# Branch projections from high and low parts, with the first gate products among the last head's products, in a two-block transformer kernel

## The chip, the cores and the metric

The kernel runs on one core of one Trainium2 chip. The metric is device time in microseconds of one execution, as the median of several runs on the same chip.

## The reference

A first block (two layers of attention of three kinds and a gated FFN) is followed by a second block with a gated linear attention (GLA) and an mLSTM side by side. All that this change touches lies in the second block, after its scans. Sequence 512, width 1024, all float32:

```python
y_gla = head_rms_norm(o_l, gla_norm_g) * silu(pp[3])
y_m = h * sigmoid(pp[8])                       # pp = split columns of u @ w_in_2
gate_gla, gate_m = split(sigmoid(pp[10]), 2)   # 2 x 1024 columns of u @ w_in_2
y = gate_gla * (y_gla @ w_br_gla) + gate_m * (y_m @ w_br_mlstm)
x = x + g1 * (y @ w_out)
x = x + g2 * swiglu(modulate(rms_norm(x, norm2_g), sh2, sc2), w_ffn_in, w_ffn_out)
return rms_norm(x, final_g)
```

## The kernel before, in words

Features lie on partitions: a 1024 x 512 activation is eight tiles of 128 x 512 (KT = 8). Most matrix products are made in three passes: each operand is split into a high part (rounded to fp32r) and a low part (value minus high), and one product of 8 tiles is 24 matmuls, high x high, high x low and low x high (`parts_steps`, `parts_job`). A product is 128 output features wide. Two products of the kernel in question are made otherwise: the branch products (`job` with raw fp32 weights and raw Y or YM).

Each engine has its own program, and engines meet at semaphores. PE writes into rings of PSUM banks: `ab` (three banks, emptied by ACT) and `db` (two banks, emptied by DVE). `fill` waits until a bank is free, `take` until it is full. `Program.more` waits for the next count of a semaphore, `do` issues an instruction and waits for it.

The mLSTM has four heads, each scanned in two directions (`mlstm_scan` on PE, `mlstm_outputs` on DVE). A scan makes row products (four partitions deep), key transposes, five state products, and four output products. In heads 0 to 2, `nxt` gives generators with the next head's projections, and `mlstm_scan` puts slices of them between its own products (`some(between, 2)`). In the last head `nxt` gives nothing. Y (GLA) and YM (mLSTM) are eight tiles each; head h makes tiles 2h and 2h + 1 of YM in `head_outputs` on DVE.

Weights of the second block come in pieces of 1 MB, in the order of the list `SECOND`, into places of SBUF given by `PLACE`. SP asks for a piece as soon as the last reader of its place has finished (`load_second`). For projection pieces POOL makes the high part (`round_piece`, L798) and DVE the low part (`second_low`, L2410). For the gate pieces and the output pieces POOL makes both (`split_piece`, L780). The raw branch weights have two halves of place 1 (`load_branch`).

After the last head, PE goes over eight output tiles m: gate product, branch product with Y, gate product, branch product with YM. ACT takes the sigmoid of the gate products, DVE multiplies, adds and splits the sum into `BR_HIGH` and `BR_LOW`. Then PE waits for all eight splits and makes the eight output products; DVE adds them to the residual x, ACT squares x, POOL folds the squares, and after the root DVE normalizes x tile by tile for the FFN (`norm_into_parts`), with high parts by ACT and low parts by DVE. For the first FFN weight ACT makes the high part after the root (`second_ffn_inputs`) and POOL the low part (`first_low`); for the second, ACT makes the high part after the eight tiles and DVE the low part.

## Time and profile before

| | |
|---|---|
| median of 3 runs | 2912.88 us (2911.32 to 2922.45) |
| the profiled execution, its own time | 2913.8 us |
| its span, first to last instruction | 2911.9 us |
| mean granted TensorE clock | 0.961 |
| PE busy | 94% of the span |
| DVE, ACT, POOL busy | 47%, 34%, 31% |

The branch stage is the stretch from about 2275 to 2467 us of the span; the last mLSTM head lies before it, from about 2217, and the third FFN starts at about 2532. A busy share is a mean over stages with different limits; the windows and the chain of waits tell them apart. A timeline row merges like instructions that follow each other; its duration is from the first start to the last end.

### The profile page before, as it was taken

The page shows a single profiled execution, that of the slowest core. Times are in us where ns is not written, and L with a number is a line of the kernel's source. Part 1 is how long each engine was busy: PE and PEld are TensorE (multiplying, and loading weights), DVE is VectorE, ACT ScalarE, POOL GpSimd, SP SyncE. Part 2 cuts the span into 40 slices and gives each one's busy share as a digit, 9 for nine tenths or more (in the row PEclk, how much of TensorE's full clock was granted, in tenths as well). Part 3 has the DMA queues.
Part 4 walks back from the last instruction along what each step waited for, and adds up shares of the span by engine and source line. Part 5 has one row for each costly group of instructions (what it writes and reads, how often), then busy time and mean ns, then how long its engine had stood idle before and what let it go on. Part 6 is the DMA issues. An engine that isn't in the chain of part 4 may idle for free.

```text
span 2911.9 us, 35929 instructions
## 1 busy us (share of the span) xinstructions
PE 2724.6 (94%) x14116; PEld 2165.0 (74%) x14116; DVE 1355.0 (47%) x1808; ACT 980.7 (34%) x1650; POOL 896.5 (31%) x674
## 2 busy tenths in 40 slices
PE   7988999999999799999998999898888999899998
PEld 6866788887798577888876767567776565688887
DVE  2748655443345776544434355545444212333332
ACT  5458522222343883222223434332222100222222
POOL 5566513345346553243461100300000223200000
PEclk8999999999999999999998999898997999899999
DMA  5220034554421101454551211011111331233332
GB/s 131 83 60 1 27 98 127 134 143 136 126 81 62 37 1 56 112 152 133 139 151 54 59 44 44 29 38 35 30 44 44 87 87 58 58 108 95 93 90 79
DMA packets 396728, 230.44 MB, mean 79 GB/s; under 512 B 9772, under 2 KB 392876, under 8 KB 396560
## 3 DMA queue, kind: packets, MB, share of 16 engines
q1 hardware_dynamic: 394608, 226.19, 28.1%
q0 software_dynamic: 1952, 1.94, 0.8%
q8 instruction: 113, 1.85, 0.3%
q14 instruction: 55, 0.45, 0.0%
HBM read 226.01 MB, written 2.10 MB: 78 GB/s over the span
## 4 chain that ended last, share of the span: by engine, by line
PE 76%; DVE 9%; ACT 8%; DMA 5%; issue 2%; POOL 1%; SPq 0%; DVEq 0%; ACTq 0%; POOLq 0%
PE ps L840 65%; PE scores L840 8%; DMA raws<-in_w_down 4%; ACT wH L1832 1%; PE ps L982 1%; DVE R L2150 1%; DVE wL L2361 1%; DVE ring_parts L2414 1%; DVE spare L2160 0%; ACT U L1671 0%; ACT R L1970 0%; DMA ring<-in_w_in 0%; DVE QK_parts L2140 0%; ACT spare L1694 0%; ACT R L1671 0%
## 5 line engine op out<-in xcount | busy, mean ns | idle before, releaser
L840 PE MATMUL ps<-xH,wH 128*128 128x512 f32 x1000 | 396.0, 396 | 7.4 <-DVE xL L2335 7.0
L840 PE MATMUL ps<-xL,wH 128*128 128x512 f32 x1000 | 390.9, 391 | 0.0
L840 PE MATMUL ps<-xH,wL 128*128 128x512 f32 x1000 | 390.5, 391 | 0.0
L1832 ACT ACTIVATE wH<-raws 128x2048 fp32r<-128x2048 f32 (+1 forms) x114 | 192.9, 1692 | 494.5 <-PE ps L840 337.0
L2361 DVE TENSOR_TENSOR wL<-raws,wH 128x2048 fp32r<-128x2048 f32 (+1 forms) x113 | 230.2, 2037 | 255.3 <-ACT wH L1832 254.6
L840 PE MATMUL ps<-ring_parts,U_parts 128*128 128x256 f32 (+1 forms) x1968 | 322.1, 293 | 21.5 <-DVE ring_parts L2217 6.2
L840 PEld LDWEIGHTS ps<-ring_parts,U_parts 128*128 128x128 f32 x1968 | 286.8, 200 | 36.8 <-issue 29.8
L840 PE MATMUL ps<-R 128*64 128x128 f32 (+3 forms) x1688 | 246.0, 336 | 32.7 <-DVE R_parts L2171 7.0
L730 POOL TENSOR_TENSOR spare<-spare,cvec 128x1024 f32<-128x1024 f32 x64 | 122.0, 1907 | 436.4 <-DMA spare<-in_w_ada 436.4
L840 PEld LDWEIGHTS ps<-R 128*64 128x64 f32 (+2 forms) x1688 | 159.6, 167 | 117.6 <-issue 62.5
L840 PEld LDWEIGHTS ps<-xH,wH 128*128 128x128 f32 x1000 | 188.8, 189 | 49.6 <-issue 8.0
L840 PE MATMUL ps<-U_parts,ring_parts 128*128 128x512 f32 (+2 forms) x720 | 216.7, 391 | 9.5 <-DVE ring_parts L2414 9.5
L840 PEld LDWEIGHTS ps<-xH,wL 128*128 128x128 f32 x1000 | 188.5, 189 | 39.9
L840 PEld LDWEIGHTS ps<-xL,wH 128*128 128x128 f32 x1000 | 188.9, 189 | 37.9 <-issue 0.5
L803 POOL CAST ring_parts<-ring 128x2048 fp32r<-128x2048 f32 x23 | 45.7, 1986 | 532.2 <-DMA ring<-in_w_in 532.0
L840 PE MATMUL ps<-hH,wH 128*128 128x512 f32 x528 | 209.3, 396 | 0.0
L840 PE MATMUL ps<-hL,wH 128*128 128x512 f32 x528 | 206.3, 391 | 0.0
L840 PE MATMUL ps<-hH,wL 128*128 128x512 f32 x528 | 206.1, 390 | 0.0
L732 POOL TENSOR_TENSOR spare<-spare 128x512 f32<-128x512 f32 (+2 forms) x192 | 188.7, 983 | 15.1
L840 PEld LDWEIGHTS ps<-U_parts,ring_parts 128*128 128x128 f32 (+1 forms) x720 | 132.8, 189 | 45.5 <-DVE ring_parts L2414 10.4
L693 POOL TENSOR_TENSOR ring_parts<-ring,ring_parts 128x2048 fp32r<-128x2048 f32 (+2 forms) x23 | 99.4, 4325 | 147.5 <-ACT ring_parts L1619 147.2
L840 PE MATMUL ps<-ring_parts 128*128 128x512 f32 (+1 forms) x376 | 131.5, 350 | 0.0
(418 smaller groups left out, 4797.4 us busy)
## 6 DMA issues: line engine op xcount, KB each, us to landing
raws<-in_w_gate_up SPq DMA_DIRECT2D x88, 512.0 KB, 5.3
ring<-in_w_in SPq DMA_DIRECT2D x34, 1024.0 KB, 5.8
spare<-in_w_ada SPq DMA_DIRECT2D x64, 512.0 KB, 3.9
raws<-in_w_down SPq DMA_DIRECT2D x32, 704.0 KB, 6.1
raws<-in_w_ffn_in SPq DMA_DIRECT2D x44, 512.0 KB, 5.0
ring<-in_w_in SPq DMA_DIRECT2D x22, 512.0 KB, 5.4
raws<-in_w_ffn_out SPq DMA_DIRECT2D x16, 704.0 KB, 4.6
ring<-in_w_o SPq DMA_DIRECT2D x12, 448.0 KB, 3.7
```

The costliest lines, as they stand in the source:

```text
L693: pg.do(nc.gpsimd.tensor_tensor(low, slot(i, KT, n_), high.bitcast(F32), ALU.subtract), piece_low)
L730: pg.do(nc.gpsimd.tensor_tensor(w_, w_, bc(cvec[:, :, ADA[a][1]], P, 2), ALU.mult))
L732: pg.do(nc.gpsimd.tensor_tensor(w[:, 0:n_ * P], w[:, 0:n_ * P], w[:, n_ * P:2 * n_ * P], ALU.add), ada_summed if n_ == 1 else None)
L803: pg.do(nc.gpsimd.tensor_copy(high, raw_), second_high)
L840: return nc.tensor.matmul(o, a, b, start=first, stop=last)
L982: ins = nc.tensor.transpose(bank[:, s_ * P:(s_ + 1) * P], PX[a % 4][:, c, s_ * P:(s_ + 1) * P], ident[:, :])
L1832: ap.do(f(wH[:, g % 2, 0:n], raws[:, g % 2, 0:n], ACT.Copy), wh_ready)
L2150: vp.do(v.tensor_reduce(nmax[:, n:n + 2], SP[a % 2][:, :, :], AX.X, ALU.max, negate=True), s_max)
L2361: vp.do(v.tensor_tensor(wL[:, g % 2, 0:n], raws[:, g % 2, 0:n], wH[:, g % 2, 0:n].bitcast(F32), ALU.subtract), wl_ready)
L2414: vp.do(v.tensor_tensor(low, raw_, high.bitcast(F32), ALU.subtract), piece_split)
```

## The change

The branch weights become pieces like the others: in `SECOND` a gate piece (`gates`, both branches' gate columns for one m) and a branch piece (columns m of both branch weights) alternate, over three places that were in use for other things before (places 0, 1 and a new place 2 in the region of the context's parts), and the output pieces follow on places 1, 3, 4 and 2. POOL only rounds all of them; DVE makes the low parts at places written out by hand. Y and YM are split: ACT makes the high parts (`y_rounds`), DVE the low parts in place (`y_subtract`), at several points of the last head.

PE's order: the four gate products of m = 0 and 1 become fillers among the last head's products; the first branch product takes the place of the first gate product; then three branch products; then for m = 2 to 7 two gate products and two branch products. The first product of the output stage waits for its tiles one by one. The first FFN weight's high part is made between the squares of tiles 6 and 7, its low part by DVE after the last residual update; the second weight's high part is made ahead of the normalized tiles.

```diff
-        PLACE = [j % 2 for j in range(N_PROJ)] + [(0, 2, 3)[j % 3] for j in range(KT + 4)]
+        SECOND += [(name, m) for m in range(KT) for name in ("gates", "branch")] + [("out", j) for j in range(4)]
+        PLACE = [j % 2 for j in range(N_PROJ)] + [2, 0, 1] + [(2, 1, 0)[j % 3] for j in range(2 * KT - 3)] + [1, 3, 4, 2]
...
@@ POOL @@
-            for j in range(SECOND.index(("gate", NH2)), N_PROJ):
+            for j in range(SECOND.index(("gate", NH2)), len(SECOND)):
                 round_piece(j)
-            for j in range(N_PROJ, len(SECOND)):
-                split_piece(j)
...
             fold_squares()
-            first_low(L)
...
@@ PE @@
+            def last_fillers(name, m=0):
+                filler = {("v", 1): (0, 0), ("v", 3): (0, 1), ("v", 4): (1, 0), ("gate", 0): (1, 1)}.get((name, m))
+                return branch_gates(*filler) if filler else iter(())
+
+            def branch(m, n):
+                columns = late_columns("branch", m, n)
+                own = m < 2 and n == 0
+                bank = SP[1][:, m, :] if own else db.fill(pe)
+                for k in range(KT):
+                    if m == 0:
+                        pe.wait_ge(y_split, n * KT + k + 1)
+                    (ah, al), (_, bh, bl) = columns(k), y_parts(n * KT + k)
+                    mm(bank[:, :], ah, bh, k == 0, False)
+                    mm(bank[:, :], ah, bl, False, False)
+                    ins = mm(bank[:, :], al, bh, False, k == KT - 1)
...
-                    nxt = projections(NH2 + h + 1) if h + 1 < NH2 else no_projections
+                    nxt = projections(NH2 + h + 1) if h + 1 < NH2 else last_fillers
...
-                    branch_gates(0, 0)
+                    branch(0, 0)
                 head_outputs()
-            pp.more(y_ready, 2 * NH2)
-            for m in range(KT):
-                if m > 0:
-                    branch_gates(m, 0)
-                pe.wait_ge(br_in[m % 2], 32 * (m // 2 + 1))
-                job(db, lambda b: b[:, :], [(branch_raw(m, 0)[:, k, :], Y[:, k, :]) for k in range(KT)])
-                branch_gates(m, 1)
-                job(db, lambda b: b[:, :], [(branch_raw(m, 1)[:, k, :], YM[:, k, :]) for k in range(KT)])
-                branch_read.append((d_full, db.n))
-            pp.more(br_ready, KT)
+            branch(1, 0)
+            branch(0, 1)
+            branch(1, 1)
+            for m in range(2, KT):
+                for n in range(2):
+                    run(branch_gates(m, n))
+                for n in range(2):
+                    branch(m, n)
             for m in range(KT):
+                j = SECOND.index(("out", m // 2))
+                parts_job(db, lambda b: b[:, :], late_columns("out", m // 2, m % 2), lambda k: (BR_HIGH[:, k, :], BR_LOW[:, k, :]),
+                          (lambda: pp.more(br_ready)) if m == 0 else None)
@@ ACT @@
                 for k in range(KT):
                     square(k)
+                    if k == KT - 2:
+                        split_high(L, 0)
                 root()
-                split_high(L, 0)
+                split_high(L, 1)
                 for k in range(KT):
                     high_tile(xH[:, k, :], k)
-                split_high(L, 1)
...
@@ ACT, after the last head @@
+            y_rounds(KT + 2, KT + 5)
+            for m in range(2):
+                ap.do(f(first_gates[m][0], first_gates[m][0], ACT.Sigmoid), gate_ready)
+            act.wait_ge(y_ready, 2 * NH2)
+            y_rounds(KT + 5, 2 * KT)
...
 DVE, mlstm_outputs(h, d), last head
+                    y_subtract(4 * d, 4 * d + 2)
                 vp.more(wexp_ready)
...
+                    if d == 1:
+                        second_low("branch", 0)
+                    y_subtract(4 * d + 2, 4 * d + 4)
                 states(mlstm_order(d), STm, DV + 1, lambda c: dec[:, d, c:c + 1])
...
@@ DVE, loop over heads @@
+                else:
+                    second_low("gates", 0)
                 for d in range(2):
                     mlstm_outputs(h, d)
+                    if h + 1 == NH2 and d == 0:
+                        second_low("gates", 1)
                 vp.also(og_ready)
+                    second_low("branch", 1)
+                    y_subtract(KT, KT + 2)
+                    head_outputs(h, 4, YM, lambda: y_subtract(KT + 2, KT + 5))
+                    y_subtract(KT + 5, 2 * KT)
...
@@ DVE, branch and output stage @@
                 split(BR_HIGH[:, m, :], BR_LOW[:, m, :], PTb[:, 0, :], br_ready)
+                if m >= 1 and m + 1 < KT:
+                    second_low("branch", m + 1)
+                    second_low(*(("gates", m + 2) if m + 2 < KT else ("out", 0)))
+            second_low("out", 1)
...
+                if m in (1, 3):
+                    second_low("out", 2 + m // 2)
+                if m == KT - 1:
+                    split_low(L, 0)
             ffn_norm(L, lambda k: gm[:, 2, k:k + 1], lambda k: mod[:, sh2 + k, 0:1])
```

## Rows read from the trace of the kernel before

**Rows 1.** The page, section 4: the chain that ended last, by engine.

```profile
PE 76%; DVE 9%; ACT 8%; DMA 5%; issue 2%; POOL 1%; SPq 0%; DVEq 0%; ACTq 0%; POOLq 0%
```

**Rows 2.** Windows: stretch, length, busy PE PEld DVE ACT POOL, granted clock, DMA, GB/s.

```profile
2133.00:2217.00 84.00, 74.98 (x395) 61.22 (x393) 36.56 (x78) 20.79 (x37) 10.73 (x4) 0.92 0.14 39
2217.00:2265.00 48.00, 40.98 (x129) 28.02 (x129) 19.59 (x51) 8.39 (x12) 0.00 (x0) 0.61 0.16 43
2548.00:2910.00 362.00, 354.18 (x1584) 293.39 (x1584) 127.35 (x127) 87.05 (x79) 0.00 (x0) 0.99 0.32 92
```

**Rows 3.** Chain of waits, branch and output stage: start, us, engine, line.

```profile
2306.60 5.45 PE scores L840 x24
...
2459.90 6.88 PE ps L840 x16
...
2467.64 4.50 DVE R L2631
...
2473.36 46.07 PE ps L840 x192
```

**Rows 4.** PE in time, last head: start, us, line, operation, count [idle before].

```profile
2222.41 2.92 PE L840 MATMUL ps<-R,C 4*128 4x512 f32 x4
...
2233.50 4.92 PE L840 MATMUL ps<-R 128*128 128x257 f32 x10 [1.15 <-ACT R L1671]
...
2264.97 0.58 PE L840 MATMUL scores<-U_parts,ring_parts 128*128 128x512 f32 x1
...
2274.82 7.13 PE L840 MATMUL ps<-R,ring 128*128 128x512 f32 x16 [1.25 <-DVEq L56]
```

**Rows 5.** PE in time, branch stage: two successive fp32 branch products.

```profile
2287.26 7.03 PE L840 MATMUL ps<-R,ring 128*128 128x512 f32 x16
...
2299.57 7.03 PE L840 MATMUL ps<-R,ring 128*128 128x512 f32 x16
```

**Rows 6.** By line: count, ns min/median/max, first and last start, form.

```profile
L2414 DVE TENSOR_TENSOR ring_parts<-ring,ring_parts x23: 2283/2293/2595, 1578.0 to 2194.2; 128x2048 fp32r<-128x2048 f32 x23
...
L803 POOL CAST ring_parts<-ring x23: 1891/1898/2533, 1560.7 to 2161.8; 128x2048 fp32r<-128x2048 f32 x23
...
L2355 DVE TENSOR_TENSOR R_parts<-R,R_parts x8: 691/692/693, 2296.3 to 2472.6; 128x512 fp32r<-128x512 f32 x8
...
L1623 ACT ACTIVATE xH<-R x24: 629/632/634, 362.4 to 2543.1; 128x512 fp32r<-128x512 f32 x24
```

**Rows 7.** DMA issues from 2150 to 2560: count, KB each, median us to landing.

```profile
R<-in_w_in SPq DMA_DIRECT2D x10, 512.0 KB, 7.0
```

**Rows 8.** PE and DVE in time, the head before the last, second direction.

```profile
2183.43 1.12 PE L840 MATMUL ps<-R,C 4*128 4x512 f32 x2
...
2193.07 0.78 PE L840 MATMUL ps<-ring_parts,U_parts 128*128 128x256 f32 x2
...
2196.80 0.60 PE L840 MATMUL ps<-R 128*128 128x257 f32 x2
...
2209.73 0.58 PE L840 MATMUL scores<-U_parts,ring_parts 128*128 128x512 f32 x1
...
2184.05 0.48 DVE L2609 TENSOR_SCALAR R<-ps,den 128x256 f32<-128x256 f32 x1
```

**Rows 9.** Windows as in group 2, three microseconds of the last head.

```profile
2229.00:2232.00 3.00, 3.00 (x15) 2.73 (x14) 0.69 (x1) 0.23 (x1) 0.00 (x0) 0.50 0.00 0
```

**Rows 10.** POOL, DVE and PE in time, start of the third FFN.

```profile
2524.68 4.50 POOL L720 TENSOR_TENSOR wL<-raws,wH 128x2048 fp32r<-128x2048 f32 x1 [7.69 <-ACT wH L1832]
...
2522.54 0.18 DVE L2107 RECIPROCAL rt<-rt 128x4 f32<-128x4 f32 x1 [2.33 <-ACTq L56]
...
2526.53 2.94 DVE L2342 TENSOR_SCALAR R<-R,mod 128x512 f32<-128x512 f32 x1
...
2530.28 0.49 DVE L2342 TENSOR_SCALAR R<-R,mod 128x512 f32<-128x512 f32 x1
...
2548.02 0.50 PE L840 MATMUL scores<-xH,wH 128*128 128x512 f32 x1 [1.26 <-DVE wL L2361]
```

More of the change, by code:

```diff
@@ L381, in build @@
         setup = sem("setup")
-        piece_in = [sem(f"piece_in{i}") for i in range(4)]
-        br_in = [sem("br_in0"), sem("br_in1")]
+        piece_in = [sem(f"piece_in{i}") for i in range(5)]
+        y_high, y_split, branch_full = sem("y_high"), sem("y_split"), sem("branch_full")
+        late_read = {}
         lr_in, gates_in = sem("lr_in"), sem("gates_in")
@@ L517, in build @@
         N_PROJ = len(SECOND)
-        SECOND += [("branch", m) for m in range(KT)] + [("out", j) for j in range(4)]
-        PLACE = [j % 2 for j in range(N_PROJ)] + [(0, 2, 3)[j % 3] for j in range(KT + 4)]
+        SECOND += [(name, m) for m in range(KT) for name in ("gates", "branch")] + [("out", j) for j in range(4)]
+        PLACE = [j % 2 for j in range(N_PROJ)] + [2, 0, 1] + [(2, 1, 0)[j % 3] for j in range(2 * KT - 3)] + [1, 3, 4, 2]
+        LOWS = SECOND[1:N_PROJ] + [("gates", 0), ("gates", 1), ("branch", 0), ("branch", 1)] + SECOND[N_PROJ + 4:]
         def place_parts(i, raw_at=None, n=256):
@@ L536, in second_dmas @@
             dst = place_parts(PLACE[j])[0]
+            if name == "gates":
+                return [(dst[:, :, n * P:(n + 1) * P], cols(w, O_BR + n * D + h * P, O_BR + n * D + (h + 1) * P)) for n in range(2)]
             if name == "branch":
[L538 removed]
+                return [(dst[:, :, n * P:(n + 1) * P], cols(A[nm][0], h * P, (h + 1) * P))
+                        for n, nm in enumerate(("w_br_gla_2", "w_br_mlstm_2"))]
             if name == "out":
@@ L1557, in _ @@
                 base = before[l]
-            last = [None] * 4
+            last = [None] * 5
             def load_second(j):
@@ L1581, in _ @@
             sp.dma_start(small_parts(LR_AT, 2 * RANK)[0], cols(A["w_in_2"][0], O_LR, O_LR + 2 * RANK)).then_inc(lr_in, 16)
-            for j in range(1, N_PROJ + 1):
+            for j in range(1, len(SECOND)):
                 load_second(j)
@@ L2034, in _, with y_rounds @@
             act.wait_ge(emc_ready, 1)
+            def y_rounds(a, b):
+                for i in range(a, b):
+                    raw_, high, _ = y_parts(i)
+                    ap.do(f(high, raw_, ACT.Copy), y_high)
             for h in range(NH2):
@@ L2038, in beside @@
                         evacuate(NH2 + h + 1, *jobs)
+                        return
+                    for job_ in jobs:
+                        if job_ in (("v", 1), ("v", 4), ("v", 3), ("gate", 0)):
+                            m, n = {("v", 1): (0, 0), ("v", 3): (0, 1), ("v", 4): (1, 0), ("gate", 0): (1, 1)}[job_]
+                            bank = ab.take(act)
+                            copy_out(first_gates[m][n], bank[:, :], a_free)
                 if h > 0:
@@ L2466, in gla_outputs, with y_subtract, head_outputs @@
                         vp.do(v.tensor_tensor(og[:, t, :], og[:, t, :], bank[:, 0:DV], ALU.add), d_free)
-            def head_outputs(h, j, dst):
+            def y_subtract(a, b):
+                for i in range(a, b):
+                    raw_, high, low = y_parts(i)
+                    vp.more(y_high)
+                    vp.do(v.tensor_tensor(low, raw_, high.bitcast(F32), ALU.subtract), y_split)
+            def head_outputs(h, j, dst, beside=None):
                 g_ = head(h)[3]
@@ L2474, in head_outputs @@
                 vp.also(og_normed)
+                if beside:
+                    beside()
                 for m in range(2):
```

108 lines of the change are left out of this document (52 added, 56 removed).

## The prediction

> **What bounds the kernel now.** I read the page first: the chain that ended last runs on PE for 76% of the span [rows 1], so time is gained only where PE does less, waits less or runs at the higher clock. The windows by stage then say which of the three applies where [rows 2]. In the last head of the second block PE is granted 0.61 of its clock, against 0.92 in the head before and 0.99 in the last FFN. The chain of waits shows the end of that block as one solid run of PE work with a single hole [rows 3]: the fp32 branch products end at 2459.90 + 6.88 = 2466.8, DVE then works alone, and PE's next row starts at 2473.36. Levels: granted 1.00 is 2.4 GHz and 0.50 is 1.2 GHz.
>
> The stretch the change rewrites runs from 2222.4 (first row product of the last head) to 2519.4 (end of the output products): 297.0 us. It divides, by [rows 3, 4], into 42.6 (the head's scans, to 2265.0), 9.85 (first gate product, head transposes and two waits, to 2274.8), 192.0 (16 branch and 15 gate products, to 2466.8), 6.6 (the hole) and 46.1 (output products).
>
> **Part 1, branch products in three passes.** One gate product, already in three passes, takes 5.45 us for 24 matmuls at the upper clock [rows 3], 227 ns each. One fp32 branch product and one gate product take 2299.57 - 2287.26 = 12.31 us [rows 5]; so a pair becomes 10.9 and saves 1.4, which over 16 pairs would be 22 us. The sum below counts jobs instead: 28 products remain behind the last head (16 branch, 12 gate), the other four gate products move into the head.
>
> The raw weights now have to be split. POOL keeps only the rounding (1.9 us per piece) and DVE takes the subtraction, 2.29 us [rows 6]. The 16 tiles of Y and YM are split too: ACT rounds 16 x 0.63 us, DVE subtracts 16 x 0.69 us [rows 6]. In a round of the branch stage (two gate and two branch products, 21.8 us) DVE has two multiplies, an add, a split and two subtractions, some 8 us by these rows: hidden behind PE. If a weight came late, the cover would be this: its place frees 10.9 us into a round, a load lands in about 7.0 us [rows 7], POOL takes 1.9, and DVE reaches it about 3 us after the round's end; it is ready some 27 us after the round began and is first read at 21.8 + 10.9 = 32.7. Margin 5.6 us, so I charge nothing. SP issues all late loads in program order, each behind a wait on the read of the piece three places back; these reads end in the same order, so none is held behind a later one.
>
> **Part 2, gate products among the last head's.** No row shows this head with fillers, so I bound it. Below: they fit wholly into holes and slow clock, and the head stays at 42.6. Above: nothing is hidden and all runs at 1.2 GHz, 42.6 + 4 x 10.9 = 86.2. The nearest rows are the second direction of the head before, which has the same products with fillers [rows 8]: 2183.43 to 2209.73, 26.3 us. From it I take away the product between transposes and states (2193.07 to 2196.80, 3.7), put in the wait for the key copies that the last head shows there, 1.15 [rows 4], and add the wider filler among the row products (512 columns for 256, so half of 5.45 more, 2.7). That is 26.4 a direction. The clock is at 0.50 as the head begins [rows 9]; the output products, which also began after a pause, took 46.1 for 43.6 and so lost 2.5 [rows 3], and I charge the same in the first direction. In the second, the DVE subtraction of the second gate piece stands between the two directions: in the head before, DVE ended the first direction's outputs at 2184.53, 1.1 us after the second began [rows 8], when PE's filler would start; it needs 2.29, so PE waits 2.3, and behind that instruction on DVE are queued the key multiplications of the second direction, which PE's transposes need. Another subtraction and two tile subtractions ahead of the states cost about 0.75, as two PSUM banks are all that PE can run ahead. For the short waits at which the clock may fall again I add 1 a direction. Together 26.4 + 26.4 + 2.5 + 2.3 + 0.75 + 2 = 60.4, nearer to the lower end since the templates have fillers.
>
> Here a rule of the pages speaks against the change. In the trace, POOL's 4.5 us subtraction ran beside a DVE scale-and-add of 0.49 us and that took 2.94 [rows 10], and the DVE add at the end of the branch stage took 4.50 [rows 3]. The Trainium skill, "SBUF — State Buffer", section "Who interferes with whom", says that a DVE instruction with two SBUF inputs is blocked for the whole of a GpSimd instruction that reads SBUF. By that rule each new DVE subtraction that starts inside a POOL rounding waits up to 1.9 us, about one such meeting (the second gate piece) on the path and +1 us; the trace's 23 subtractions beside those roundings keep within 2.283 to 2.595 us [rows 6], and I charge nothing.
>
> **Part 3, the joint of head and branch stage.** A branch product takes the place of the gate product there; the next one needs only the older Y tiles, so the wait of 1.25 before the first branch product [rows 4] goes: 9.85 - 1.25 = 8.6. What is late next is the split of the last YM tiles: after the head's normalization DVE subtracts three tiles, gates two and subtracts three more behind ACT's roundings, some 6.5 us; PE has the transposes, a whole product (5.45) and five older tiles (3.4) to go before it reads them. Covered by some 3 us; if not, PE waits for the excess.
>
> **Part 4, output products by tile.** The hole of 6.6 us goes, as seven of eight tiles are ready and the eighth follows in 2.5 us (add, cast, subtraction, no POOL beside them), against 4.8 us (seven eighths of 5.45) of products on the others. The output products start at the upper clock: 8 x 5.45 = 43.6 for 46.1. Their weights: the second piece is asked for when the last Y product ends, lands about 7, is split by 6 to 10 after the stage's start and is read at 10.9; thin but enough.
>
> **Part 5, third FFN's first weights.** POOL's subtraction leaves; the scale-and-add falls from 2.94 to 0.49, and the whole norm chain, which PE follows tile by tile, moves 2.45 ahead. The second weight's high part is made before the norm tiles, so its subtraction follows the last tile at once and most of PE's 1.26 wait [rows 10] goes: 1.05. The subtraction that DVE takes over (2.29) fits between the last residual update and the root, 2.33 us in which DVE waits now [rows 10]. Nothing after that changes: the FFN runs at 0.99 [rows 2].
>
> **The sum.** After: 60.4 (head), 8.6 (joint, with one branch product), 27 x 5.45 = 147.2 and 43.6 make 259.8, for 297.0: 37.2 less. With part 5's 3.5: 40.7. The profiled execution took 2913.8 (span 2911.9 and 1.9 around it), 0.9 above the median of the runs: 2913.8 - 40.7 = 2873.
>
> **Rivals.** (a) The clock stays at 1.2 GHz through the last head. For it: in 2229 to 2232 PE was busy 3.00 of 3.00 us and still granted 0.50 [rows 9]; against: those are products with 4 rows, and the head before, with fillers, had 0.92 [rows 2]. Price: the head at 86.2, time 2873 + 25.8 = 2899. The Trainium skill, "TensorE: Matmul & The Clock Gate", section "What's actually happening", has activity release the throttle; this row shows a busy engine that stays throttled, so the rule alone does not exclude (a). (b) DVE becomes the last head's bound: 4 x 2.29 + 16 x 0.69 = 20.2 us of new work in its program order. For it: the states wait behind it; against: DVE is busy 19.6 of 48 us there [rows 2]. If none is hidden, 20.2 - 3.05 already counted: 2890. (c) Slower than before: the late pieces share three places, so a load can't be asked for ahead. The decision point is the landing: with L for it, a branch piece is in time while L is under 32.7 - 10.9 - 1.9 - 2.3 = 17.6 us; beyond it each of six rounds loses the excess. To end 0.5% above before, 55 us must go, 9.2 a round, L near 27. The median of ten such loads is 7.0 [rows 7]. (d) The change does less than it says: fillers or splits stall so that only parts 4 and 5 and half of part 1 are left, 13 + 3.5 + 9 = 25: 2888. (e) Better: no low clock and no wait for the second gate piece in the head, 2 x 26.4: 60.4 - 52.8 = 7.6 less, 2865.
>
> **How the numbers follow.** About 0.5% (15 us) is what a measurement of this kernel can tell from no change. Forecast 0.68 (2868 to 2881), (e) 0.10, (b) and (d) 0.14 together, (a) 0.06, (c) 0.02. The range runs from 2863 to 2889, so that (a), (c) and about half of (b), (d) and a little of (e) stay outside. Faster by over 0.5% means under 2899: all but half of (a), and (c): 0.94; same 0.04; slower 0.02.
>
> **What would show it.** Right: no fp32 branch matmuls, products of 5.45 us back to back from the joint to the end of the output products; the last head of about 60 us with a granted clock near 0.85; PE's wait of some 2.3 us for DVE between its two directions; no hole before the output products; the scale-and-add at 0.49. Wrong: PE waiting for DVE or DMA inside the branch stage, a granted clock of 0.6 in the last head, DVE the releaser of most of its waits, or the splits of the last YM tiles late at the joint.

## The result: 2894.8 us, 0.75% faster than before and 22 us slower than forecast

| | before | after |
|---|---|---|
| median (range, 8 runs each) | 2914.24 us (2911.32 to 2922.45) | 2894.80 us (2887.74 to 2908.35) |
| ratio after / before | | 0.9925, interval 0.9901 to 0.9948 |
| the profiled execution, its span | 2913.8, 2911.9 us | 2887.74, 2885.9 us |
| mean granted TensorE clock | 0.961 | 0.964 |

The forecast was 2873 (2863 to 2889). In the profiled execution 15 us are missing, in the median 7 more. The profile after, in the order of the prediction's views. First the windows (length, busy PE PEld DVE ACT POOL, granted clock, DMA, GB/s) of the head before the last, of the last head's two directions, of the branch stage and of the output products, against [rows 2]:

```profile
2135.10:2220.10 85.00, 76.12 (x392) 62.73 (x393) 36.58 (x73) 19.12 (x35) 7.81 (x4) 0.90 0.18 50
2225.40:2259.80 34.40, 29.99 (x106) 20.84 (x105) 11.48 (x28) 9.10 (x14) 1.28 (x1) 0.80 0.12 31
2259.80:2296.70 36.90, 30.68 (x103) 21.90 (x104) 17.38 (x33) 4.70 (x8) 1.89 (x1) 0.77 0.11 29
2306.80:2454.00 147.20, 147.20 (x651) 121.83 (x651) 59.19 (x57) 11.86 (x20) 22.87 (x13) 1.00 0.34 93
2454.00:2497.20 43.20, 43.20 (x194) 35.80 (x192) 15.47 (x14) 6.35 (x8) 16.32 (x9) 1.00 0.34 98
```

The two last rows are close to the forecast (190.8 us): PE is busy in all 190.4 us and at the full clock in all of them. The two rows ahead are the miss: 71.3 us of head for a forecast of 60.4. The chain of waits shows the joint, and behind it one unbroken run of products (start, us, what; the answer to [rows 3]):

```profile
2298.49 2.30 DVE spare_parts L2434
2300.82 2.27 DVE R_parts L2492
...
2303.84 0.19 DVE rsg L2497
...
2305.68 1.10 PE ps L1363 x8
2306.78 5.48 PE scores L836 x24
2312.26 32.64 PE ps L836 x144
...
2442.81 54.41 PE ps L836 x240
```

PE in time, the last head (start, us, line, operation, count, [idle before <- what ended it]), against [rows 4, 8]:

```profile
2225.45 2.07 PE L836 MATMUL ps<-R,C 4*128 4x512 f32 x2
2243.58 1.22 PE L836 MATMUL ps<-R 128*128 128x257 f32 x2 [3.15 <-ACT R L1669]
2264.11 0.80 PE L836 MATMUL scores<-U_parts,ring_parts 128*128 128x512 f32 x1 [3.21 <-DVE ring_parts L2434]
2280.92 1.23 PE L836 MATMUL ps<-R 128*128 128x257 f32 x2 [1.87 <-ACT R L1669]
2305.68 1.10 PE L1363 MATMUL ps<-ident,R 128*128 128x128 f32 x8 [3.12 <-DVEq L56]
```

Four waits of 1.9 to 3.2 us. The windows show what follows the second of them, the one between the two directions: PE busy 8.89 of 9.00 us, at 1.2 GHz:

```profile
2264.00:2273.00 9.00, 8.89 (x20) 6.32 (x21) 1.32 (x4) 0.00 (x0) 0.00 (x0) 0.50 0.00 0
```

And two DVE instructions with the POOL casts that they met, in time:

```profile
2161.53 1.90 POOL L802 CAST ring_parts<-ring 128x2048 fp32r<-128x2048 f32 x1 [20.00 <-DMA ring<-in_w_in]
2161.59 2.38 DVE L2591 SCALAR_TENSOR_TENSOR R<-R,convw 128x512 f32<-128x512 f32 x1
...
2260.02 1.89 POOL L802 CAST U_parts<-spare 128x2048 fp32r<-128x2048 f32 x1 [33.33 <-DMA spare<-in_w_br_mlstm]
2260.92 3.13 DVE L2434 TENSOR_TENSOR ring_parts<-ring,ring_parts 128x2048 fp32r<-128x2048 f32 x1
```

Account of the profiled execution, measured minus forecast: the start of the last head 2225.45 - 2222.41 = +3.0; the head 71.3 - 60.4 = +10.9; the joint (2296.75 to 2306.78) 10.0 - 8.6 = +1.4; branch and output products -0.3; the FFN's start -0.3. Together +14.7 of the 14.7 that are missing.

### The profile page after: what moved, and what is told of

Read it like the earlier page. It is cut to its first block, busy times and chain, and to the rows that moved or that the text cites. A ratio compares the mean times of both kernels' runs of the same rounds, so it can differ in the third digit from the quotient of the medians.

```text
span 2885.9 us, 36282 instructions
## 1 busy us (share of the span) xinstructions
PE 2699.2 (94%) x14244; PEld 2186.4 (76%) x14244; DVE 1407.8 (49%) x1845; ACT 992.7 (34%) x1670; POOL 856.3 (30%) x669
## 3 DMA queue, kind: packets, MB, share of 16 engines
q1 hardware_dynamic: 394608, 226.19, 28.3%
q8 instruction: 114, 1.87, 0.3%
## 4 chain that ended last, share of the span: by engine, by line
PE 75%; DVE 9%; ACT 8%; DMA 5%; issue 2%; POOL 0%; SPq 0%; DVEq 0%; ACTq 0%; POOLq 0%
PE ps L836 64%; PE scores L836 9%; DMA raws<-in_w_down 4%; PE ps L978 1%; ACT wH L1830 1%; DVE R L2171 1%; DVE wL L2381 1%; DVE ring_parts L2434 1%; DMA ring<-in_w_in 0%; ACT U L1669 0%; ACT spare L1692 0%; ACT R L1697 0%; DMA R<-in_x 0%; DVE spare L2181 0%; ACT R L1669 0%
## 5 line engine op out<-in xcount | busy, mean ns | idle before, releaser
L836 PE MATMUL ps<-ring_parts,U_parts 128*128 128x256 f32 (+2 forms) x2000 | 334.3, 294 | 24.6 <-DVE ring_parts L2238 6.7
L802 POOL CAST ring_parts<-ring 128x2048 fp32r<-128x2048 f32 x34 | 67.8, 1993 | 687.1 <-DMA ring<-in_w_in 614.4
L836 PE MATMUL ps<-U_parts,ring_parts 128*128 128x512 f32 (+2 forms) x768 | 230.6, 390 | 9.5 <-DVE ring_parts L2434 9.5
L836 PEld LDWEIGHTS ps<-U_parts,ring_parts 128*128 128x128 f32 (+1 forms) x768 | 142.1, 189 | 47.0 <-DVE ring_parts L2434 10.4
L836 PE MATMUL ps<-ring_parts 128*128 128x512 f32 (+1 forms) x400 | 141.7, 354 | 0.0
```

What stands on the lines that cost most here:

```text
L802: pg.do(nc.gpsimd.tensor_copy(high, raw_), second_high)
L836: return nc.tensor.matmul(o, a, b, start=first, stop=last)
```

## The experiments

All runs are compared by one stretch, from the last head's first row product to the head transposes (the part of the account that missed): 80.2 us after the change. The forecast puts it at 60.4 + 8.6 - 1.1 (the transposes) = 67.9. The stretch is read from one profiled execution of each run, the time is the median of all its executions, and the ratio is to the kernel before on the same chip. The changed kernel was measured three times, and its stretch was 80.2, 80.0 and 85.0; e10, which changes nothing in the last head, shows 84.0. A difference of under some 5 us in the stretch is therefore not shown by a single profile.

| run | stretch, us | time, us (range) | ratio to before, interval |
|---|---|---|---|
| changed, as above | 80.2 | 2894.8 (2887.7 to 2908.4) | 0.9925, 0.9901 to 0.9948 |
| e4_changed_again | 80.0 | 2890.2 (2889.9 to 2895.3) | 0.9899, 0.9870 to 0.9928 |
| e14_changed_third | 85.0 | 2892.4 (2881.3 to 2907.4) | 0.9914, 0.9887 to 0.9942 |
| e1_no_fillers | 76.6 | 2882.6 (2881.6 to 2884.2) | 0.9868, 0.9845 to 0.9891 |
| e2_second_gate_split_early | 70.8 | 2884.4 (2877.5 to 2887.8) | 0.9871, 0.9844 to 0.9898 |
| e3_fillers_after_transposes | 69.5 | 2877.9 (2874.8 to 2879.8) | 0.9851, 0.9827 to 0.9875 |
| e5_idle_filled | 73.9 | 2885.4 (2882.8 to 2887.3) | 0.9876, 0.9843 to 0.9908 |
| e7_exp_table_early | 79.6 | 2900.0 (2884.9 to 2915.8) | 0.9922, 0.9889 to 0.9956 |
| e8_narrow_splits | 75.2 | 2885.4 (2878.5 to 2902.2) | 0.9885, 0.9840 to 0.9930 |
| e9_all | 66.8 | 2871.9 (2871.6 to 2896.1) | 0.9851, 0.9801 to 0.9900 |
| e13_all_again | 67.8 | 2881.3 (2869.9 to 2891.7) | 0.9884, 0.9846 to 0.9922 |
| e11_joint_mended | 64.4 | 2876.3 (2872.7 to 2879.8) | 0.9872, 0.9841 to 0.9903 |
| e17_mended_again | 64.4 | 2873.4 (2869.3 to 2880.9) | 0.9848, 0.9819 to 0.9876 |
| e12_casts_in_quarters | 84.2 | 2904.5 (2877.3 to 2908.4) | 0.9939, 0.9910 to 0.9967 |
| e15_fillers_between_short_rows | 78.4 | 2910.0 (2905.6 to 2914.7) | 0.9972, 0.9955 to 0.9989 |
| e16_mended_and_between | 64.5 | 2893.1 (2888.4 to 2898.7) | 0.9911, 0.9883 to 0.9939 |
| e10_output_waits_for_all | 84.0 | 2896.6 (one run) | |

**Are the fillers, one subtraction or DVE's whole work at fault?** Four kernels were measured side by side on one chip; e4_changed_again is the changed kernel unedited.

e1_no_fillers: the four gate products run in a row behind the scans.

```diff
-                filler = {("v", 1): (0, 0), ("v", 3): (0, 1), ("v", 4): (1, 0), ("gate", 0): (1, 1)}.get((name, m))
+                filler = None
...
                 else:
+                    for m in range(2):
+                        for n in range(2):
+                            run(branch_gates(m, n))
                     branch(0, 0)
```

> The four gate products leave the last head and run behind its scans, where they cover the wait for the head's normalization; all splits by ACT and DVE stay where they are. Theory A (the last head took 71.3 us instead of 60.4 because PE waits there and falls to 1.2 GHz after each wait): the head without fillers goes back to about 43 us, with 21.8 us of gate products behind it and no 3.1 us wait before the head's transposes, so 7 to 10 us less than the changed kernel. Theory B (the new DVE work is the bound of the head): the scans keep at least 55 us and the kernel is 5 us or more slower than the changed one. Theory C (the shortfall lies outside the last head): within 3 us of the changed kernel.

e2_second_gate_split_early: the second gate piece's subtraction behind the key multiplications of direction 0 instead of between the directions.

```diff
                 vp.do(v.scalar_tensor_tensor(kdm[:, 256:768], k_[:, 256:768], scale, bank[:, :], ALU.mult, ALU.mult), d_free)
+                if h + 1 == NH2 and d == 0:
+                    second_low("gates", 1)
...
-                    if h + 1 == NH2 and d == 0:
-                        second_low("gates", 1)
```

> The DVE subtraction of the second gate piece moves from between the two directions to behind the first key multiplication of the first direction, where DVE waited 4.5 us for PE. Theory A: PE's wait of 4.5 us between the directions goes, and with it the fall of the clock there (12.1 us for row products and filler go back to about 9), so 6 to 8 us less than the changed kernel. Theory B: DVE does the same work, so within 2 us. Theory C: within 2 us.

e3_fillers_after_transposes: the two fillers among the row products move behind the key transposes, where PE waits for the key copies.

```diff
-                filler = {("v", 1): (0, 0), ("v", 3): (0, 1), ("v", 4): (1, 0), ("gate", 0): (1, 1)}.get((name, m))
+                filler = {("v", 2): (0, 0), ("v", 3): (0, 1), ("v", 5): (1, 0), ("gate", 0): (1, 1)}.get((name, m))
```

> Two of the four gate products move from among the row products to behind the key transposes, where PE waits for ACT's copies (3.15 and 1.87 us in the changed kernel); the second gate piece is then needed later, so the wait between the directions goes too. Theory A: the waits are covered, the head falls by 6 to 10 us. Theory B: within 2 us of the changed kernel or slower. Theory C: within 2 us.

> The changed kernel as it is, on the same chip as the three others. All theories: a median of 2889 to 2898 us. Theory A: its last head (first row product to first branch product) again takes 70 us or more with a granted clock near 0.8, and a slower execution is slower there. Theory C: the head differs by under 2 us between executions and the spread lies elsewhere.

Each of the three edits was faster than the changed kernel beside it (2890.2): by 7.7, 5.9 and 12.3 us. These times hold the other heads too, which differ between executions (in e3's profile the head before the last takes 81.9 us, in e4's 88.0, for a reason given further on), so the stretch is the better measure. Windows as above. e1: the scans alone, then the four gate products:

```profile
2225.90:2275.00 49.10, 38.63 (x112) 25.81 (x112) 27.96 (x59) 11.43 (x18) 1.13 (x1) 0.62 0.00 1
2275.00:2296.90 21.90, 21.90 (x98) 18.11 (x98) 4.10 (x8) 5.43 (x13) 1.90 (x1) 1.00 0.18 49
```

The two directions of e2:

```profile
2222.70:2257.00 34.30, 29.95 (x105) 20.84 (x104) 13.73 (x28) 9.12 (x14) 1.11 (x1) 0.80 0.11 31
2257.00:2285.30 28.30, 25.23 (x105) 18.27 (x105) 14.36 (x33) 4.71 (x8) 1.90 (x1) 0.94 0.15 38
```

The two directions of e3:

```profile
2228.00:2258.30 30.30, 29.08 (x105) 21.97 (x104) 11.46 (x27) 9.12 (x14) 1.17 (x1) 0.78 0.13 35
2258.30:2289.40 31.10, 26.83 (x103) 20.64 (x104) 17.40 (x33) 4.72 (x8) 1.90 (x1) 0.84 0.13 35
```

e2 changes nothing in the first direction (34.3 for 34.4) and takes 8.6 us from the second (28.3 for 36.9), though the wait it removes was 3.2 (the expectation wrote 4.5; the trace has 3.21): the clock there goes from 0.77 to 0.94. PE's idle time in that window falls by 3.15 us (6.22 to 3.07) and its busy time, over the same products, by 5.45 (30.68 to 25.23). Against all three profiles of the changed kernel the second direction is 8.1 to 8.8 us shorter. So a wait of 3.2 us cost some 8.6. e3 keeps PE at work in three of the waits of the changed kernel; a new wait of 3.05 for DVE among the row products of the second direction remains.

e1 came out between the expected numbers. The scans take 49.1 us, where theory A had 43 and theory B at least 55. Of the 6.5 above the 42.6 of before, 4.7 are two waits for DVE in the second direction that the kernel before does not have; the exponential's table load, explained below, adds 1.3.

```profile
2252.97 2.15 PE L836 MATMUL ps<-R,C 4*128 4x512 f32 x4 [2.23 <-DVE R L2616]
2265.36 3.10 PE L836 MATMUL ps<-R 128*128 128x257 f32 x6 [2.49 <-DVE R L2472]
```

Scans and gate products together take 71.0 us, where the changed kernel's head takes 71.3: as the change places them, the fillers gain nothing there. The 3.6 us by which e1's stretch is shorter is about the wait of 3.12 at the head transposes, which the four products now cover (no idle time stands in front of the transposes):

```profile
2302.48 0.71 PE L1363 MATMUL ps<-ident,R 128*128 128x128 f32 x5
```

**Is it the wait or the clock behind it?** e5_idle_filled keeps PE at work in the same waits with products that nothing needs.

```diff
                 key_transposes(kdm)
                 transposed = ab.n
+                if h + 1 == NH2:
+                    for _ in range(10):
+                        mm(SP[1][:, 1, :], x_high(0)[:, 0:P], x_high(0), True, True)
...
+                if h + 1 == NH2 and d == 1:
+                    for _ in range(18):
+                        mm(SP[1][:, 1, :], x_high(0)[:, 0:P], x_high(0), True, True)
```

> Adds matmuls that no result needs: 18 of 512 columns ahead of the last head's second direction, 10 behind the key transposes of each direction, where TensorE waits for ACT and DVE. The stretch from the head's first row product to the head transposes is 80.2 us in the changed kernel (80.0 in its second profile). Theory A1, most of the loss is the 1.2 GHz that follows each wait: the added work lies inside the waits (3.2, 3.2 and 1.9 us) but for some 2 to 5 us, the granted clock of the second direction rises from 0.68 to over 0.9, and the low-clock loss of some 7 us behind its start falls away: stretch 75 to 79, time 2884 to 2889. Theory A2, the waits themselves are the loss, the clock only follows: stretch 82 to 86, time 2892 to 2896.

With 38 more matmuls the stretch is 6 us shorter, below the range of either theory. The directions:

```profile
2229.90:2262.00 32.10, 30.17 (x111) 21.11 (x110) 10.42 (x23) 9.11 (x14) 1.10 (x1) 0.83 0.11 32
2262.00:2298.00 36.00, 34.84 (x147) 26.36 (x147) 20.23 (x42) 5.30 (x11) 3.52 (x2) 0.95 0.12 32
```

The second direction (its window runs some 2 us into the branch product) is granted 0.95 instead of 0.77. PE was kept busy in these waits with work that nothing needs, and the stretch still became shorter: so the low clock behind the waits is a cost of its own. In e2 it was the larger part (5.45 us of busy time against 3.15 of waiting).

**Two smaller suspects.** e7_exp_table_early: ACT loads a table ahead of an exponential. In the kernel before this load of the last head stood ahead of ACT's wait for the exponents; in the changed kernel, with the roundings of four Y tiles in between, it stands behind that wait. Before, then after:

```profile
2223.28 1.28 ACT L2051 ACT_TABLE_LOAD   x1
2231.77 0.63 ACT L2051 ACTIVATE R<-R 128x512 f32<-128x512 f32 x1 [7.21 <-DVEq L56]
...
2240.56 1.28 ACT L2064 ACT_TABLE_LOAD   x1 [2.21 <-DVEq L56]
2241.85 0.63 ACT L2064 ACTIVATE R<-R 128x512 f32<-128x512 f32 x1
```

```diff
                             y_rounds(0, 4)
+                            ap.do(f(unused[:, :], eps[:, :], ACT.Exp))
```

> One 128 x 1 exponential on ACT behind the first four roundings of Y tiles, so that the exponential's table is loaded before ACT waits for the exponents (the load took 1.28 us behind that wait in the changed kernel). Theory A: the wait of the first direction's state products falls from 3.15 to some 1.9 us, all of it on the path: stretch from the head's first row product to the head transposes 80.0 to 78.5, time some 2889. Rival: the keys wait for DVE anyway, the load was hidden: wait 3.15 and stretch 80 as before.

The wait fell from 3.15 to 1.88 as expected. The stretch is 79.6, 0.4 to 0.6 less, which is within the spread of the unedited kernel: that the load alone shortens the head is not shown. e8_narrow_splits takes nearly all of DVE's new work away, so its results are not those of the kernel; it is there for its time alone.

```diff
+                if (name, h) in (("gates", 0), ("gates", 1), ("branch", 0), ("branch", 1)):
+                    raw_, high, low = raw_[:, 0:1, 0:8], high[:, 0:1, 0:8], low[:, 0:1, 0:8]
...
-                    raw_, high, low = y_parts(i)
+                    raw_, high, low = [t[:, 0:8] for t in y_parts(i)]
```

> Leaves out nearly all subtraction work that the change gave DVE in the last head: the low parts of the first two gate pieces, the first two branch pieces and all 16 tiles of Y and YM are made on 8 columns only, and the products read the high parts twice instead; TensorE, ACT, POOL and the loads keep all their work and all waits stay. Theory A (one subtraction stands at the wrong place; the sum of DVE's work doesn't matter): the wait of 3.2 us between the directions goes, with it what the run with that split moved ahead gained, and the wait of 2.3 to 3.1 at the head transposes goes: stretch 67 to 70 us, time 2878 to 2882. Theory B (DVE's whole new work of 20 us holds the head up): stretch under 64, all waits for DVE gone, time under 2874.

75.2: neither theory's number. The wait between the directions shrank to 1.12 and did not go (the piece stays queued behind the first direction's outputs), and the second direction's clock rose only from 0.77 to 0.80. So 20 us of DVE work less gave some 5 us, no more than the spread, and moving one of those instructions gave 9.4: in this head the place of DVE's work in its queue counts for more than its amount. It is not free even so, as the 4.7 us of waits in e1 show.

**Do the gains add?** e9_all joins e2, e3 and e7; e11_joint_mended also makes the second branch piece's low part in the second direction and loads the square root's table ahead of ACT's wait for the head's outputs. e13 and e17 are the same two kernels again.

```diff
-                    second_low("branch", 1)
                     y_subtract(KT, KT + 2)
...
                     y_subtract(4 * d + 2, 4 * d + 4)
+                    if d == 1:
+                        second_low("branch", 1)
...
+                if h + 1 == NH2:
+                    ap.do(f(unused[:, :], eps[:, :], ACT.Sqrt))
                 head_norm(mlstm_squares)
```

> Three edits at once: the second gate split ahead of the second key multiplication's end, the exponential's table early, the fillers behind the transposes instead of among the row products. Theory A: their gains add where they meet different waits: stretch from the head's first row product to the head transposes 65 to 68 us instead of 80, time 2870 to 2876. If all three gain by the same clock fall: stretch 69, time 2877, no better than the fillers alone.

> The three edits of the run with all three, and two at the joint: the second branch piece's low part is made by DVE in the second direction instead of ahead of the head's normalization, and ACT loads the square root's table (1.28 us) ahead of its wait for the head's outputs. The wait at the head transposes was 2.20 us there: DVE's reciprocal came 0.65 us after ACT's root, ACT's root 1.3 us late by the table. Theory A: the wait falls to some 0.3 to 0.5 us, the stretch from the head's first row product to the head transposes from 66.8 to 65, time 1.8 us below the run with all three, some 2870. Rival (the split moved into the second direction delays the states): the stretch stays at 66 to 68.

> The run with all three edits once more (early second gate split, exponential's table early, fillers behind the transposes), whose profiled execution had its last head start 21 us later than the changed kernel's while its three other executions took 2871.5 to 2871.9. Theory A: the late start came from stretches ahead of the last head and is not the kernel's; stretch from the last head's first row product to the head transposes 66 to 68 us, time 2870 to 2874. Rival: it comes again with this kernel: time 2885 to 2896.

> The run with the joint mended once more, for its interval: stretch from the last head's first row product to the head transposes 64 to 66 us (80 in the changed kernel), time 2870 to 2880, some 15 us below the changed kernel of the same call, which is the shortfall of the forecast 2873.

They add in part. Alone, e2, e3 and e7 gained 9.4, 10.7 and 0.6 us of the stretch, 20.7 in all; together 13.4 (66.8) and 12.4 (67.8), as e2 and e3 both remove the wait between the directions. That is theory A's range of 65 to 68. With the joint mended it is 64.4 twice. In e17 the wait at the joint is 0.35:

```profile
2282.53 5.82 PE L836 MATMUL scores<-R_parts,ring_parts 128*128 128x512 f32 x24
2288.70 1.10 PE L1363 MATMUL ps<-ident,R 128*128 128x128 f32 x8 [0.35 <-DVEq L56]
```

2873.4 is 19 us below the changed kernel beside it (2892.4) and 0.9848 of before, with e9 (0.9851) and e3 (0.9851) the lowest ratio here. That it equals the forecast of 2873 is in part luck: its stretch is 3.5 us shorter than the forecast's 67.9. e13's last head starts late again, as its rival had it, though its time of 2881.3 lies between the two theories; the next runs take this up.

**Why does the changed kernel's time spread?** e14 is the changed kernel; its profile fell on a long execution (2907.0). e12_casts_in_quarters shortens the POOL casts that DVE can meet. e15_fillers_between_short_rows moves the last filler tiles in between the row products of 4 rows and 128 columns, in all heads; e16 does so in e11's kernel.

```diff
-                pg.do(nc.gpsimd.tensor_copy(high, raw_), second_high)
+                quarters = 4 if j >= SECOND.index(("gate", NH2)) else 1
+                for a in range(0, KT, KT // quarters):
+                    b = a + KT // quarters
+                    pg.do(nc.gpsimd.tensor_copy(high[:, a:b, :], raw_[:, a:b, :]), *([second_high] if b == KT else []))
```

```diff
-                run(between)
                 bank = db.fill(pe)
                 for j in range(TT):
+                    some(between, 1)
                     mm(bank[:, j * P:(j + 1) * P], sel, rE[d][:, j * P:(j + 1) * P], True, False)
...
+                run(between)
```

> The changed kernel, unedited, beside the next three runs. In the profiled executions so far the three heads ahead of the last take 91.7, 81.9 and 81.9 to 88.0 us from transposes to transposes, or 94.1, 88.7 and 88.7 in three executions of other kernels, where the granted clock falls to 0.50 for some 11 us in each direction instead of 3.4. Theory A: the spread of its executions (2887.7 to 2908.4) is these two lengths: executions fall in groups near 2888 to 2891 and 6 to 20 us above. Rival: a spread without groups, from all stretches.

> The changed kernel with POOL's roundings of the later pieces in four quarters of some 0.5 us each instead of one of 1.9. Theory: DVE waits out a POOL rounding that started first. Then in the head before the last no DVE instruction takes over 1.3 us where one took 2.38 of 0.75, the PE wait of 1.33 there goes and that head takes 81.9 us from transposes to transposes instead of 85.0 or 88.0; the second gate piece's subtraction takes at most 2.8 instead of 3.13, time 2882 to 2889 with less spread. Rival (the lengths come from the shared port at any size, or the four starts each collide): head at 85 or more, no gain.

> The changed kernel with the last three tiles of the filler product moved from ahead of each direction's eight short row products (4 rows, 128 columns) to between them, in all heads; no work is added. The granted clock falls to 0.50 during or right behind these row products although TensorE is busy all the time. Theory A: the row products in a row are what the fall follows: it comes later or not at all, heads 0 to 2 take 79 to 82 us and never 88.7, the last head's stretch to the transposes falls from 80 to 76 to 79, time 2880 to 2887 with less spread. Rival: the fall stays where it is, heads 82 to 88.7, time as the changed kernel's.

> The run with the joint mended, and the fillers between the short row products of heads 0 to 2 (the last head's fillers stand behind the transposes there). Theory A: heads 0 to 2 never at 88.7, time 2866 to 2874. Rival: as the run with the joint mended, 2872 to 2880.

Windows of the two heads ahead of the last, in e14's profile:

```profile
2057.20:2145.90 88.70, 81.15 (x392) 67.45 (x392) 34.95 (x73) 19.09 (x35) 5.87 (x3) 0.85 0.13 36
2145.90:2234.50 88.60, 79.72 (x392) 65.38 (x392) 36.56 (x73) 19.14 (x35) 7.75 (x4) 0.87 0.17 48
```

The same 392 matmuls take 82.0 us in the changed kernel's first profile, at 0.92 ([rows 2] has that for before). There is no new wait in the first of these heads: PE is busy longer at the lower clock. In steps of three microseconds (busy PE, granted clock, DMA, GB/s):

```profile
2084.00:2087.00 3.00, 3.00 (x16) 1.00 0.00 0
2087.00:2090.00 3.00, 3.00 (x15) 0.59 0.00 0
2090.00:2093.00 3.00, 3.00 (x15) 0.50 0.01 3
2093.00:2096.00 3.00, 3.00 (x16) 0.50 0.00 0
2096.00:2099.00 3.00, 3.00 (x19) 0.71 0.00 0
```

PE never stopped, and for some 10 us it ran at 1.2 GHz. In e11's profile, whose head takes 81.9 us, the same fall lasts less than 4:

```profile
2081.40:2085.40 4.00, 4.00 (x27) 1.00 0.01 2
2085.40:2089.40 4.00, 4.00 (x23) 0.57 0.00 0
2089.40:2093.40 4.00, 4.00 (x32) 1.00 0.00 0
```

That is why the last head starts late in e14, e9 and e13 (heads of 94.1, 88.8 and 88.6 us in e14, against 91.8, 82.0 and 85.0 in the first profile). Of the 19.2 us by which e14's profiled execution is longer than the first one, 12.8 lie in these three heads and 4.7 in the last head's stretch. So theory A holds for most of the place, but the ten executions of e14 form a row from 2881 to 2907 and not clear groups. What decides between the two lengths stays open. My guess, the row products that follow each other, fell: with tiles between them (e15) the heads took 97.8, 88.4 and 93.0 us and every execution was above 2905; e16 likewise took 20 us more than e17 with the same 64.5 in the last head. e12 shows the other part: the meeting of 2.38 us shrank to 1.15 and PE's wait of 1.33 went, but its profiled heads were the long ones and its ten executions lie in two groups, three at 2877 to 2882, seven at 2898 to 2908; no gain in time is shown, so the quarters are no remedy.

**Was the hole one cause or two?** e10_output_waits_for_all:

```diff
+            pp.more(br_ready, KT)
             for m in range(KT):
                 j = SECOND.index(("out", m // 2))
...
-                          (lambda: pp.more(br_ready)) if m == 0 else None)
+                          None)
```

> One part undone: TensorE waits for all eight split sums ahead of the output products, as the kernel before did. Before, the hole there was 6.6 us, of which the DVE add beside POOL's subtraction was 4.50; the same add takes 0.69 where POOL is idle. Theory A (two causes, the wait for all tiles and POOL's subtraction): hole 6.6 - 3.8 = 2.8 us, and the output products, which begin after a pause again, take 44 to 46 us instead of 43.2; from the end of the branch products to the end of the output products 46.5 to 49 instead of 43.5. Rival (the wait for all tiles was the whole hole): hole near 6.6, the stretch 50 to 53.

The chain:

```profile
2456.56 0.70 DVE R L2681
...
2457.39 1.61 DVE R L2683
...
2460.24 45.37 PE ps L836 x192
```

Hole 3.7 us for an expected 2.8 (the add met a POOL cast, 1.61 for the 0.69 I assumed), products 45.4, both together 49.1 against 43.5 with the tile-wise wait and 6.6 + 46.1 = 52.7 before. Two causes, each read from one execution: the wait by tile gives 5.6, POOL's subtraction gone 3.6.

## Why the prediction missed, step by step

**Parts 1, 4 and 5 were right.** A product takes 5.44 us (32.64 for six), as [rows 3] said; PE has no wait in the whole branch stage, so no weight came late and rival (c) never came near. The output products take 43.5 from the last branch product on, without a hole. The FFN's scale-and-add takes 0.49, and the second weight's first product starts 24.8 us after the output products, against 28.6 before: 3.8 for my 3.5.

**Part 2 is the step that failed**: the price of PE's waits in the last head, 60.4 us forecast and 71.3 measured. Three of its terms were too small.

The waits for the key copies: I set 1.15 in each direction, and they were 3.15 and 1.87, together 2.7 more. The 1.15 of [rows 4] had been read where PE ran at 0.50. At that clock PE's transposes take longer, and less of the wait is left behind them. The second direction of e10, the same program up to there, shows this: PE was at 0.50 and waited 1.21, while in the profile after it was at 1.00 ahead of its wait of 1.87. From the first transpose to the next product both took 2.7 to 2.8 us. (First e10's window and wait, then the window after; columns as above.)

```profile
2281.00:2284.00 3.00, 1.79 (x9) 1.18 (x7) 2.39 (x4) 1.67 (x4) 0.00 (x0) 0.50 0.00 0
2283.96 0.79 PE L836 MATMUL ps<-R 128*128 128x257 f32 x1 [1.21 <-ACT R L1670]
...
2274.50:2279.50 5.00, 4.54 (x30) 3.61 (x28) 1.23 (x3) 0.91 (x2) 0.00 (x0) 1.00 0.00 0
```

The other 1.28 of the 3.15 is the table load that the change put behind ACT's wait (e7). Second, the wait for the second gate piece was sized 2.3 and measured 3.2. Third, and above all, the clock: "For the short waits at which the clock may fall again I add 1 a direction", and e2 puts a single wait of 3.2 us at 8.6. The forecast had priced waits by their length. Of the 10.9 us that the head is longer, the first two terms make 3.6. The remaining 7.3 is put down to the clock by subtraction, so that some 11.8 us stand where 4.5 had been charged for it (2.5 and twice 1). This is an estimate, as the 0.75 for the other subtractions was never measured by itself.

[rows 9] had shown this price, PE busy at 0.50, and rival (a) had used it for the whole head only. The truth lay between: 0.80 and 0.77 in the two directions, where I had forecast about 0.85. So rival (a) had a part of the mechanism and was too dear; (b), priced at 17 us, fell with e8, where taking that work away gave some 5. (d) had the size (2888, the profiled execution's 2887.7), but by luck: the parts it gave up came true, and its sum does not follow from the parts, whose own numbers (9.1 for part 4, 3.5 for part 5, 11 for half of part 1) make 23.6, or 2890.

Beside [rows 9] stands the Trainium skill, "TensorE: Matmul & The Clock Gate", section "What's actually happening": activity releases the throttle. The 10 us at 0.50 with PE busy in e14 show that a busy PE alone did not do so here. The section also says that the moment of the transition varies from run to run of one kernel. The two head lengths would fit that; no run here shows it to be their reason.

**What I charged at nothing beside POOL** was not nothing. I had read the 23 subtractions of [rows 6] as standing beside the roundings. In time, 22 of them run beside no POOL cast at all, and the one that does began first (2.29 us, the cast 2.03): the row could not speak against the rule. The second gate piece's subtraction did begin inside a cast, 0.9 us after its start, and took 3.13 for 2.29, which is the +1 us that I had left out. In the head before the last the order of two starts decided: here the cast began at 2161.53 and DVE's instruction at 2161.59, and DVE took 2.38 for 0.75; before the change DVE was first, by 0.22, and POOL waited:

```profile
2161.61 0.75 DVE L2563 SCALAR_TENSOR_TENSOR R<-R,convw 128x512 f32<-128x512 f32 x1
...
2161.83 2.28 POOL L803 CAST ring_parts<-ring 128x2048 fp32r<-128x2048 f32 x1 [20.23 <-DMA ring<-in_w_in]
```

That head became 3.1 us longer. It is not the change's doing in any of its lines: both kernels have this cast. Two other runs show the order at work. In e8 DVE began 0.40 us ahead of the cast, in e3 it had ended (rows below); DVE took 0.75 in both, and the head 81.9 us as before the change:

```profile
2167.22 0.75 DVE L2591 SCALAR_TENSOR_TENSOR R<-R,convw 128x512 f32<-128x512 f32 x1
2168.35 1.90 POOL L802 CAST ring_parts<-ring 128x2048 fp32r<-128x2048 f32 x1 [21.14 <-DMA ring<-in_w_in]
```

In all other profiles of the changed kernel and its variants the two began within 0.15 us of each other, nearly always the cast first (in e17 DVE's record is 0.05 us ahead); e12's quarters aside, DVE took 2.3 to 2.5 there, and the head 84.9 us or more. The Trainium skill, "SBUF — State Buffer", section "Who interferes with whom", says that a DVE instruction with two SBUF inputs contends with a GpSimd instruction that reads SBUF, and that the order of issue decides who is blocked; the prediction had left the second half out. The meetings here agree with it (DVE 3.13 and 2.38 where the cast was first, POOL 2.28 where DVE was), e12's 1.15 too.

**Part 3, the joint.** I had counted the splits behind the head's normalization and overlooked those ahead of it: the second branch piece (2.30) and two tiles (2.99, one beside a cast) stand in DVE's queue in front of the reciprocal that PE's transposes need. PE waited 3.12. e11 moved the piece, and ACT's table load with it, and 0.35 was left.

**The median's 7 us above the profiled execution** are long heads as far as the profiles show: the profile that I built the sum on had short ones, and e14's, of a long execution, has long ones in all four heads. The executions that make the median were not profiled themselves. What sends a head into the long form, and whether the changed kernel does so more often than the kernel before, is open: in e14's comparison 4 of 21 executions of before and 4 of 10 of the changed kernel lie 8 us or more above their median, too few to tell.

## What to carry to other kernels

Price a wait of PE by what the clock does behind it, from a stretch of the same trace that begins after such a wait: here 3.2 us of waiting cost 8.6. Filler products are worth their place in the waits, not in between products that already keep the engine busy. When work is given to an engine, follow each instruction that then stands behind it in that queue, to the one that the critical engine needs next.

## What the runs showed of the hardware

TensorE fell to 1.2 GHz while its record is busy throughout, and stayed there under 4 us in one execution and some 10 us in another, in the same part of the same head; a whole head of 392 matmuls took 82.0 or 88.7 us by that. Matmuls that compute nothing needed made the last head faster (e5: stretch 80.0 to 73.9). The 1.28 us table load of ACT stood ahead of the wait of the activation that needs it in the kernel before and behind it in the changed kernel; a dummy activation ahead of the wait takes it off the path (wait 3.15 to 1.88). A DVE instruction that begins 0.06 us after a POOL cast took 2.38 us for 0.75, and the cast took 2.28 for 1.90 where DVE began 0.22 us earlier.
